# The running sum of squares of two norms, moved from VectorE to GpSimd behind its weight splits

## What is computed

```
def rmsnorm(x, g):
    xf = x.astype(jnp.float32)
    xf = xf * lax.rsqrt(jnp.mean(xf * xf, axis=-1, keepdims=True) + EPS)
    return (xf * g.astype(jnp.float32)).astype(x.dtype)

def conv_ffn(x, buf, w_up, conv_w, conv_b, w_down):
    u = x @ w_up
    ...
    val, gate = uc[..., :D_FF], uc[..., D_FF:]
    return (jax.nn.gelu(gate) * val) @ w_down, new_buf

        x = x + y
        y, fbuf = conv_ffn(rmsnorm(x, p['norm_ffn'][l]), ffn_buf0[l], p['ffn_w_up'][l],
                           p['ffn_conv_w'][l], p['ffn_conv_b'][l], p['ffn_w_down'][l])
```

## Time and profile before

| what | us |
| --- | --- |
| median of three runs | 2536.71 |
| the profiled execution's own time | 2535.36 |
| its span, first to last instruction | 2533.5 |
| PE busy | 2487.9 (98%) |
| DVE busy | 1733.7 (68%) |
| ACT busy | 1066.0 (42%) |
| POOL busy | 861.5 (34%) |
| TensorE clock granted, mean | 0.995 of full speed |

### The profile page before, as it was taken

How to read it: one execution, slowest core, us unless ns; L and a number is a source line. 1 busy time by engine, 2 the same in 40 slices (tenths; PEclk the granted TensorE clock), 3 DMA queues, 4 the chain that set the end, 5 groups by cost and what they waited for, 6 DMA issues and landing times.

```text
span 2533.5 us, 41794 instructions
## 1 busy us (share of the span) xinstructions
PE 2487.9 (98%) x16316; PEld 2428.1 (96%) x16316; DVE 1733.7 (68%) x2810; ACT 1066.0 (42%) x1846; POOL 861.5 (34%) x533
## 2 busy tenths in 40 slices
PE   8999989999999999999999999998999999999998
PEld 8999989999999999998999999898999999999998
DVE  8877487666666666776656655648766666666678
ACT  5655253333333333334444444624433333333333
POOL 2001333444433333343333333032344443343341
PEclk9999999999999999999999999999999999999999
DMA  4112211111111111143233322311111111111112
GB/s 144 49 44 73 97 34 51 51 51 51 51 49 44 51 47 43 46 144 120 95 95 100 103 95 91 151 59 34 51 51 51 51 47 47 50 46 42 48 47 97
DMA packets 102769, 170.16 MB, mean 67 GB/s; under 512 B 11909, under 2 KB 50309, under 8 KB 102318
## 3 DMA queue, kind: packets, MB, share of 16 engines
q1 hardware_dynamic: 96622, 145.19, 17.9%
q10 hardware_dynamic: 5952, 22.30, 2.3%
HBM read 145.93 MB, written 26.23 MB: 68 GB/s over the span
## 4 chain that ended last, share of the span: by engine, by line
PE 86%; DVE 9%; ACT 2%; issue 2%; POOL 1%; DMA 1%; DVEq 0%; SPq 0%; ACTq 0%; POOLq 0%
PE psum L1366 19%; PE psum L1232 12%; PE psum L1234 12%; PE psum L1233 11%; PE psum L1118 9%; PE psum L1425 3%; PE psum L1429 3%; PE psum L1427 3%; PE psum L1459 2%; PE psum L1483 2%; PE psum L1099 2%; PE psum L1471 2%; PE psum L1662 1%; PE psum L1178 1%; DVE line L2777 1%
## 5 line engine op out<-in xcount | busy, mean ns | idle before, releaser
L743 POOL TENSOR_TENSOR w_lo<-w_raw,w_hi 128x512 fp32r<-128x512 f32 x236 | 373.6, 1584 | 789.6 <-ACT w_hi L1784 789.3
L1232 PE MATMUL psum<-xn_hi,w_hi 128*128 128x352 f32 x1536 | 498.8, 325 | 13.7 <-DVE line L2750 8.3
L1234 PE MATMUL psum<-xn_lo,w_hi 128*128 128x352 f32 x1536 | 498.4, 324 | 0.0
L1233 PE MATMUL psum<-xn_hi,w_lo 128*128 128x352 f32 x1536 | 497.1, 324 | 0.0
L1784 ACT ACTIVATE w_hi<-w_raw 128x512 fp32r<-128x512 f32 x300 | 188.2, 629 | 553.5 <-DVE w_raw L2613 318.1
L1366 PE MATMUL psum<-h_hi,w_hi 128*128 128x352 f32 x1032 | 332.3, 322 | 2.3 <-DVE x L2708 2.1
L1366 PE MATMUL psum<-h_hi,w_lo 128*128 128x352 f32 x1032 | 333.2, 323 | 0.0
L1366 PE MATMUL psum<-h_lo,w_hi 128*128 128x352 f32 x1032 | 332.3, 322 | 0.0
L1232 PEld LDWEIGHTS psum<-xn_hi,w_hi 128*128 128x128 f32 x1536 | 290.6, 189 | 16.7 <-DVE line L2750 8.9
L1234 PEld LDWEIGHTS psum<-xn_lo,w_hi 128*128 128x128 f32 x1536 | 292.1, 190 | 0.0
L1233 PEld LDWEIGHTS psum<-xn_hi,w_lo 128*128 128x128 f32 x1536 | 291.2, 190 | 0.0
(11 more groups left out here) (358 smaller groups left out, 5565.9 us busy)
## 6 DMA issues: line engine op xcount, KB each, us to landing
w_raw<-in_w SPq DMA_DIRECT2D x190, 256.0 KB, 2.7
w_raw<-in_w SPq DMA_DIRECT2D x56, 512.0 KB, 3.5
w_raw_third<-in_w SPq DMA_DIRECT2D x98, 256.0 KB, 2.9
k_pages<-in_cache_k SPq DMA_DIRECT2D x128, 64.0 KB, 1.9
v_pages<-in_cache_v SPq DMA_DIRECT2D x128, 64.0 KB, 2.0
scratch_line<-scratch_row ACTq DMA_DIRECT2D x1, 4608.0 KB, 21.0
x<-in_x SPq DMA_DIRECT2D x8, 528.0 KB, 8.4
scratch_x<-x ACTq DMA_DIRECT2D x1, 4224.0 KB, 12.5
```

The source lines that it names most:

```text
L743: return eng.tensor_tensor(out_lo, op_src(op), out_hi.bitcast(F32), ALU.subtract).then_inc(FS[l][LOW[op][0]], 1)
L1232: pe.matmul(out, op_hi(op)[:, k, :], hi, start=start, stop=False, skip_group_check=True)
L1233: pe.matmul(out, op_lo(op)[:, k, :], hi, start=False, stop=False, skip_group_check=True)
L1234: return pe.matmul(out, op_hi(op)[:, k, :], lo, start=False, stop=True, skip_group_check=True)
```

## The change

In both passages the 7 adds leave DVE and are made by POOL. The adds k = 1 to 5 stand each behind the split of one of the units 3 to 7. The adds k = 6 and 7 stand together behind the splits of b11 and b21 and ahead of the low part of b22. The other norms keep their adds on DVE.

```diff
@@ gpsimd
+            def add_square(r, k):
+
+                pool.wait_ge(sq_done, KT * r + k + 1)
+                if k > 1:
+                    pool.wait_ge(sum_done, (KT - 1) * r + k - 1)
+                pool.tensor_tensor(Z[2][:, 0:T], squares(r, 0) if k == 1 else Z[2][:, 0:T], squares(r, k), ALU.add
+                                   ).then_inc(sum_done, 1)
+
+            def outs_and_squares(u0, r):
+
+                for j in range(3, KT):
+                    straight(u0 + j, u0 + j + 1)
+                    add_square(r, j - 2)
+
             def ffn(l, a_end):
                 for op in OP:
                     if l and op[0] == "d" and op[1] == GROUPS - 1:
                         break
+                    if OP[op] == EARLY:
+                        add_square(2 * l + 1, KT - 2)
+                        add_square(2 * l + 1, KT - 1)
                     if OP[op] < EARLY:
                         pool.wait_ge(acc_done, a_end - 1)
                     if not on_dve(op):
@@ gpsimd, layer 0
             pool.wait_ge(w_lo, U_OUT + 3)
-            straight(U_OUT + 3, U_OUT + 4)
-            straight(U_OUT + 4, U_OUT + KT)
+            outs_and_squares(U_OUT, 1)
             ffn(0, A_OUT + KT)
@@ gpsimd, layer 1
             pool.wait_ge(w_lo, whole(U_O + 2))
-            straight(U_O + 3, U_O + KT)
+            outs_and_squares(U_O, 3)
             ffn(1, A_O + KT)
@@ vector, norm_after_units
                         first_sums(l, 0)
-                    add_square(r, k)
                     if l and k == 4:
@@ vector, norm_after_units
                 weight_low(l, ("b12", 0))
-                add_square(r, KT - 1)
                 for s in (2, 1, 3):
                     s_low(3, s)
```

## The result

The changed kernel takes 2542.43 us, the median of 12 runs (2540.0 to 2544.5), against 2536.39 us for the kernel before in 12 runs (2535.66 to 2537.33): ratio 1.0023, 95% interval 1.0015 to 1.0031. It is slower by 6.0 us. The prediction said 2543.6, between 2538.5 and 2547.5.

The account below looks back on a forecast made before the run. The prediction took the reciprocal's start in each passage to bound the kernel; 2 x 2.6 for the two layers plus 1.7 for the clock made +6.9 us, on the median 2536.71 giving 2543.6 us, range 2538.5 to 2547.5.

Parts of the forecast that it names:

- What bounds: Passage into the feed-forward layer: whatever moves the reciprocal's start, set by DVE's line and ACT's root, moves the kernel's end.
- Part 1: Adds 1 to 5 on POOL cost 0 us, covered by the 11 us PE needs for each output tile.
- Part 2: Add 6 on POOL takes a turn in DVE's unbroken line and delays all up to `add_to_x` 7: +1.1 us.
- One of the things named as showing it: A sign of being right: the `ends_low` behind L2618 lasts about 2.0 us for 0.94.
- Part 3: Add 7 on POOL delays the low part of b12 by 0 to 4.4 us; the reciprocal starts 2.6 us later.
- The second bound: By DVE's own line `third_sum` starts at 339.2 for 337.35, +1.85 us, the lower bound of the layer.
- Part 4: PE's clock falls behind the new wait before b12, delaying the sum: 0 to +1.7 us a layer, taken for one layer.
- not slower: Rival, 10%: POOL's add does not hold DVE, the reciprocal starts 1.2 to 2.2 us earlier; about 2533.3 us.
- DVE keeps its turn: Rival, 15%: DVE keeps its turn while it has work queued, `third_sum` 1.65 us late; +3.3, 2540.0 us.
- The clock falls in both layers: Rival, 20%: the fall of the clock comes in both layers; +8.6, 2545.3 us.
- Hidden whole: Rival, 8%: PE's 4.21 us wait before the scaled products takes the whole delay up; 2536.7 us.

Follow-up runs that it names:

- e1_first_five: Changed kernel with only adds 1 to 5 on POOL, adds 6 and 7 back on DVE at their old places: 2536.09 us, 2536.27 before.
- e3_six_only: Changed kernel with only add 6 on POOL, the other adds on DVE at their old places: 2538.30 us, 2536.27 before.
- e4_seven_only: Changed kernel with only add 7 on POOL, the other adds on DVE at their old places: 2540.70 us, 2536.27 before.
- e5_pool_reads: Kernel before, plus an extra POOL add with unread result at the places of adds 6 and 7, two a layer: 2545.26 us, 2535.81 before.
- e10_pe_sum_five_on_pool: Changed kernel without adds 6 and 7, PE summing three lines over the partitions instead; adds 1 to 5 on POOL: 2532.37 us, 2536.37 before.
- e7_late_on_dve: Kernel before, all adds on DVE, with adds 6 and 7 moved behind `s_low(3, ...)`, ahead of `third_sum`: 2535.20 us, 2535.81 before.
- e9_seven_behind_b22: Changed kernel with add 7 one place later on POOL, behind the low part of b22: 2540.35 us, 2536.37 before.
- e6_pool_writes: Kernel before, plus two POOL memsets, which read nothing, at each of the places of adds 6 and 7: 2535.20 us, 2535.81 before.

## Why the prediction was right

The sign, the place and the size of the main term were right.

- **What bounds.** The start of the reciprocal carries the time, as said: it moves by 2.75 us in layer 0 and by 6.06 in layer 1, which contains layer 0's part; within each passage 2.62 and 2.61. One reading was off: before the change the root did not stand behind PE's sum but behind its table load and `third_sum`, and the sum had 0.95 us to spare. The forecast did not suffer, since it counted the 1.32 us of the root from the later end of the sum, which is what now sets it.
- **Part 1, adds 1 to 5 at 0.** Right, by e1_first_five.
- **Part 2, add 6 at +1.1.** The last add to `x` moved by 1.19, less the 0.13 by which the execution was later already: 1.06. The reciprocal of e3_six_only moves by 1.5 in layer 0, less the 0.42 us by which that execution was later before the place, 1.07; the kernel by 2.0 for both. One of the things named as showing it was miscalculated: the `ends_low` behind L2618 was to last about 2.0 us for 0.94, but from its issue at 314.2 to 0.94 - 0.15 behind POOL's 316.56 it is 3.2. It lasted 3.16 us.
- **Part 3, the low part of b12 at 336.9, the sum's end at 342.7, the reciprocal at 344.0 to 344.1.** Measured: 336.79, the root's start behind it at 342.83, 344.15. All three of POOL's turns fell where I put them, t2's among them. The price of one add, 2.47 us, also holds where POOL is not held: 2.67 at 329.22 with 0.2 us of waiting. The second bound, DVE's own line, was 339.2 for `third_sum`; measured 339.11. Behind it the line gained 1.1 us that were not forecast, since the four `s_low` took 1.82 us for 2.92 with POOL's next piece waiting, and it was through at 342.13, 2.0 us ahead of the root.
- **Part 4, the clock.** This term was mis-sized and misplaced for this kernel. I put +1.7 us for one more fall of the clock before the sum, in one layer. No such fall came in the profiled execution. It does exist: in layer 1 of e4_seven_only, behind a wait for b12 of 2.60 us, and in layer 0 of e5_pool_reads, behind one of 2.72, PE takes 7.51 us to the end of the sum, for 5.94 in the changed kernel, and the 1.57 us are near the forecast 1.7. What came in the changed kernel is a fall at another place. Two windows after the reciprocal, and one inside the second, in the changed kernel and in the kernel before:

```profile
345.00:357.00 12.00, 8.70 (x53) 8.16 (x52) 11.53 (x15) 2.82 (x7) 1.30 (x1) 1.00 0.16 54
365.00:377.00 12.00, 9.07 (x47) 8.79 (x46) 8.40 (x13) 6.32 (x10) 4.09 (x3) 0.86 0.22 66
372.80:376.00 3.20, 3.11 (x11) 3.11 (x12) 2.05 (x3) 1.60 (x3) 1.55 (x1) 0.50 0.22 66
```

```profile
345.00:357.00 12.00, 7.79 (x40) 7.51 (x39) 11.49 (x18) 2.96 (x4) 2.78 (x3) 0.86 0.08 22
365.00:377.00 12.00, 10.43 (x64) 10.14 (x64) 8.37 (x13) 6.75 (x10) 5.10 (x3) 1.00 0.27 86
```

Before, the clock was 0.86 in the first window, behind PE's wait of 4.21 us. With the change that wait is 3.30 us, the first window is at 1.00 and the second at 0.86. The last row of the changed kernel tells where: from 372.80 to 376, behind the new 2.92 us of waiting for ACT's copy, the granted clock is 0.50, and the matmuls there take 0.49 us for 0.32. That the shorter wait moved the fall is not shown: behind the same 3.31 us in layer 0 of e4_seven_only and e10_pe_sum_five_on_pool the first window is at 0.86.

What came on behind the reciprocal: the wait for the copy ends 2.93 us later than before (372.89 for 369.96), and the first product of the feed-forward's second half (`h_hi`) starts 3.26 later (403.18 for 399.92). Of the 3.26, 0.13 is the later start, 2.62 the passage, and 0.51 is added behind the reciprocal, in layer 1 0.57: 1.1 us in all, for the predicted 1.7. Between the copy and `h_hi` the fall shows up as 0.3 us only; 0.5 us for which PE idled there before are gone, and the rest of the 1.7 that 3.4 us at half clock cost is not accounted for. Nor is the 1.1 surely the clock's: in e3_six_only, with that window at 1.00 in both layers, the stretch from the reciprocal to `h_hi` is also longer than before, by 0.1 us in layer 0 and 0.4 in layer 1. No run set the clock.

The sum was 2 x 2.6 + 1.7 = 6.9. The measured one is 2 x 2.6 + 1.1, the 0.13 of the later start and 0.2 between the layers, less some 0.3 us that is gained behind 1802.8: +6.3 in the span, and +6.0 in the medians. The main term was foreseen with its mechanism; that the last one, 1.7, met a 1.1 of another origin is luck. The wider spread of the changed kernel's runs (4.5 us against 1.7) may come from where the clock falls in each; only one execution of each kernel shows that, so this stays open.

Of the rivals, "not slower" is refuted by e5_pool_reads (POOL's reading does hold DVE), and "DVE keeps its turn" by the profile after, where it matters: at 329.22 POOL came in behind one instruction. At other places DVE did keep it (last section). "The clock falls in both layers" did not happen ahead of the sum, in the one execution that was profiled. "Hidden whole" would have needed PE's 4.21 us wait to take the delay up; it gave 0.9 us and the end moved all the same.

## What to carry to other kernels

Moving an instruction with two SBUF inputs from DVE to POOL freed nothing where DVE's line had no idle time and consisted of such instructions: it was paid there at POOL's duration (2.5 us) in place of DVE's (1.24 us), and each further POOL instruction that slid into the line cost nearly its own length (1.1 us for 1.28). It was free only in DVE's idle time, and then there was nothing to gain either (e1_first_five). Such a move can also hand the end of the chain to another engine, here from DVE's line to PE's sum, so work out both. And ask which third engine idles while the two contend: here PE took over both adds, mostly inside its own waits, and with a clock that did not fall there the kernel became 3 to 4 us faster.

## What the runs showed of the hardware that was not expected

- A POOL instruction often waits for the one DVE instruction that runs, but not always. For the low part of t2 it took 3.19 us for 1.28 in the kernel before, 3.20 at 331.58 in e7_late_on_dve, and 2.03 at 335.99 in e9_seven_behind_b22, each time behind two to four DVE instructions that followed one another without idle time. The low part of t3 did the same in the changed kernel (2.67 at 340.59). Beside similar instructions at 329.22 in the changed kernel POOL waited 0.2 us. What decides is not settled.
- The memset of 128x1056 on POOL takes 1.0 us (two in 2.03) and does not hold DVE's add beside it (1.25 us), where an add of the same size takes 2.5 us and does (3.56).
- Where the clock falls is not fixed by PE's waits alone. With waits of 0.42, 1.65 and 0.58 or 0.59 us the window of 321 to 333 us is at 0.86 in the kernel before and at 1.00 in e6_pool_writes. The changed kernel has as many falls in each passage as the kernel before, two of about 3.4 us at half clock, one of them at another place.
